# Hyena long convolution: filter quarters in four banks, decays made a step ahead, copies and loads moved

## What is computed

```python
def bidir_long_conv(z, h_fwd, h_bwd, bias):
    L = z.shape[1]
    k = jnp.concatenate([h_fwd, jnp.zeros_like(h_fwd[:1]), h_bwd[1:][::-1]], axis=0)
    kf = jnp.fft.rfft(k.astype(jnp.float32), n=2 * L, axis=0)
    zf = jnp.fft.rfft(z.astype(jnp.float32), n=2 * L, axis=1)
    y = jnp.fft.irfft(zf * kf, n=2 * L, axis=1)[:, :L]
    return (y + z.astype(jnp.float32) * bias).astype(z.dtype)

def hyena_mixer(h, ...):
    u = short_conv(h @ w_in + b_in, conv_w, conv_b)
    x1, x2, v = jnp.split(u, 3, axis=-1)
    filt = hyena_filters(L, ...)          # sin-MLP times exp(-t * |deltas|)
    z = v
    for n, gate in enumerate((x1, x2)):
        z = gate * bidir_long_conv(z, filt[:, n, 0], filt[:, n, 1], fbias[n])
    return z @ w_out + b_out
```

## Time and profile before

| | us |
|---|---|
| median of 3 runs | 3601.22 (3597.62 to 3602.07) |
| the profiled execution, its time | 3599.02 |
| its span, first to last instruction | 3597.4 |
| first matmul of the long convolution | 391.94 |
| first matmul of M(0,0), M(1,0), M(2,0) | 452.80, 567.60, 680.56 |
| third tile of the output projection begins | 1012.12 |

### The profile page before, as it was taken

One profiled execution on the slowest core, in us unless ns is written; L12 is line 12 of the kernel. 1 busy time (PEld: TensorE's weight loads), 2 busy tenths in 40 slices (PEclk: granted clock), 3 DMA queues, 4 the chain that ended last, 5 costly groups with the idle time before them and its releaser, 6 DMA issues.

```text
span 3597.4 us, 49991 instructions
## 1 busy us (share of the span) xinstructions
PE 3287.9 (91%) x19458; PEld 2568.9 (71%) x19458; DVE 2141.1 (60%) x3189; ACT 1304.9 (36%) x2141; POOL 312.3 (9%) x508
## 2 busy tenths in 40 slices
PE   7999788888798999999899889999999979999797
PEld 4888445554576788888687757777777758888685
DVE  6999634343356555554677655555556576665676
ACT  3221333333234433333345443333334253333344
POOL 0111234444200000000000200000000000000000
PEclk8999989998899999999999999999999989999999
DMA  7555644567621322222634410000001133333632
GB/s 290 205 199 200 212 120 137 161 179 153 201 75 59 129 85 80 82 94 105 218 100 144 152 54 8 15 7 7 7 25 59 65 102 106 103 103 111 220 100 88
DMA packets 183696, 410.14 MB, mean 114 GB/s; under 512 B 33263, under 2 KB 60207, under 8 KB 180791
## 3 DMA queue, kind: packets, MB, share of 16 engines
q1 hardware_dynamic: 131288, 270.56, 22.7%
q0 software_dynamic: 51936, 131.27, 12.4%
q10 hardware_dynamic: 288, 5.77, 0.4%
HBM read 262.38 MB, written 81.00 MB: 95 GB/s over the span
## 4 chain that ended last, share of the span: by engine, by line
PE 76%; DVE 12%; DMA 4%; ACT 3%; issue 3%; POOL 1%; SPq 1%; DVEq 0%; ACTq 0%
PE ps L655 19%; PE ps L657 19%; PE ps L656 19%; PE ps L2487 3%; PE ps L2327 3%; PE ps L2461 2%; PE ps L2422 2%; PE ps L2440 2%; PE ps L725 1%; DVE mx L2859 1%; PE ps L2362 1%; PE ps L2522 1%; DMA traw<-hidden_scratch 1%; PE ps L2496 1%; DVE pts L2840 1%
## 5 line engine op out<-in xcount | busy, mean ns | idle before, releaser
L655 PE MATMUL ps<-HB,gsp 128*128 128x512 f32 x1232 | 488.7, 397 | 37.3 <-DVE HB L831 22.0
L656 PE MATMUL ps<-HB,gsp 128*128 128x512 f32 x1232 | 484.9, 394 | 0.0
L657 PE MATMUL ps<-HB,gsp 128*128 128x512 f32 x1232 | 483.7, 393 | 0.0
L1109 DVE TENSOR_TENSOR gsp<-graw,gsp 128x512 fp32r<-128x512 f32 x330 | 226.5, 690 | 262.3 <-ACT gsp L1088 261.5
L1088 ACT ACTIVATE gsp<-graw 128x512 fp32r<-128x512 f32 x330 | 206.6, 628 | 325.5 <-PE ps L657 266.1
L655 PEld LDWEIGHTS ps<-HB,gsp 128*128 128x128 f32 x1232 | 234.3, 190 | 90.6 <-issue 21.5
L655 PE MATMUL ps<-tsp,wdh 128*128 128x512 f32 x616 | 243.6, 396 | 36.6 <-DVE tsp L1366 36.6
L657 PEld LDWEIGHTS ps<-HB,gsp 128*128 128x128 f32 x1232 | 234.1, 190 | 49.9
L656 PEld LDWEIGHTS ps<-HB,gsp 128*128 128x128 f32 x1232 | 234.7, 190 | 46.6 <-issue 1.0
L656 PE MATMUL ps<-tsp,wdh 128*128 128x512 f32 x616 | 242.1, 393 | 0.0
L657 PE MATMUL ps<-tsp,wdh 128*128 128x512 f32 x616 | 242.0, 393 | 0.0
(11 more groups left out here) (278 smaller groups left out, 7498.4 us busy)
## 6 DMA issues: line engine op xcount, KB each, us to landing
graw<-in_w_gu SPq DMA_DIRECT2D x176, 256.0 KB, 2.7
mring<-in_mod_w POOLq DMA_DIRECT2D x78, 512.0 KB, 4.5
hidden_scratch<-R SPq DMA_DIRECT2D x154, 256.0 KB, 2.4
traw<-hidden_scratch SPq DMA_DIRECT2D x154, 256.0 KB, 2.6
t2k<-s POOLq DMA_DIRECT2D x80, 256.0 KB, 5.6
t2z<-s POOLq DMA_DIRECT2D x160, 128.0 KB, 6.0
t2w<-w POOLq DMA_DIRECT2D x160, 128.0 KB, 3.3
wd<-in_w_dx SPq DMA_DIRECT2D x6, 2816.0 KB, 14.7
```

Of the source, the lines that this page charges most:

```text
L655: pe.matmul(o, wh, xh, start=start, stop=False, skip_group_check=onto)
L656: pe.matmul(o, wh, xl, start=False, stop=False, skip_group_check=onto)
L657: return pe.matmul(o, wl, xh, start=False, stop=stop, skip_group_check=onto)
L1109: dve.tensor_tensor(gsp[U % 3][:, 1, :], graw[:, q, W_SLOT[i], :], gsp[U % 3][:, 0, :].bitcast(F32), ALU.subtract).then_inc(w.lo, 1)
```

## The change

- **Four A banks.** The first pair of a K step is in banks 0 and 1, its second pair in 6 and 7. PE waits for the last use of the bank in hand (A_FREE) and no longer for all tiles before a pair. M(it,1) takes its two spectrum sets in the other order (0, 6).
- **Decays ahead.** `dec` has four buffers. ACT makes all four decays of a quarter in the step after the K step before it (B, Z or M), behind the copies that are due there, or, where two K steps follow one another, at the head of the second. In a K step it then copies all held transforms.
- **Order on PE.** In Z steps that find a held filter quarter, two transposes come ahead of the filter's transforms; each signal transform is one place later, and up to two are carried into the next K step. In B steps the held transforms come behind two parts of B, not one.
- **Spectrum copied by two engines.** ACT copies the parts 0 and 2 of S, DVE the parts 1 and 3 (semaphore `s_kd`).
- **Last short convolution.** It moves behind DVE's tiles of K(0,1), the two reductions behind those of K(0,0); of twelve half reductions four stay in K(0,2) and K(0,3), eight go behind S(0,0).
- **Tail.** `mix_raw` is loaded once S(4,1) is computed, ahead of B(4,0); `gbuf` after the weights; the loads of `R` wait until the last `t2w` has landed. Four of the eight `mix_x_low` steps of DVE move into M(4,1).

`mix_raw` goes ahead of `gbuf`. The core of the diff:

```diff
+            for x in range(n["A"], n["A"] + 4 if kind in "KZB" else 0):
+                u = x - n["A"]
+                A_BANK.append(6 * (u // 2) + u % 2 if kind == "K" else u % 2)
+                A_FREE.append(a_last[A_BANK[x]])
+                a_last[A_BANK[x]] = x + 1
...
-        BANK_A, SETS_B = (0, 1), (4, 2)
-        SETS_C, SETS_D, SETS_S = ((4, 2), (6, 0)), ((6, 0), (4, 2)), (4, 6)
+        SETS_B = (4, 2)
+        SETS_C, SETS_D, SETS_S = ((4, 2), (0, 6)), ((6, 0), (4, 2)), (4, 6)
...
+            def decays(quarter):
+
+                it, o = quarter // 4, quarter % 4
+                kb = it if it < NCH else NCH + o
+                act.wait_ge(s_jl[kb % 2], 48 * (kb // 2 + 1))
+                for u in range(4):
+                    ku = 4 * quarter + u
+                    at = NBX + u if it == NCH else ku % 16
+                    if ku >= 4:
+                        act.wait_ge(s_ae, KA_AT[ku - 4] + 1)
+                    act.activation(dec[ku % 4][:], dlt[kb % 2][:, 0:CW], ACT.Exp, scale=nt[:, at:at + 1]).then_inc(s_dec, 1)
...
-                if au >= 2:
-                    pe.wait_ge(s_ae, au - 1)
+                if A_FREE[au]:
+                    pe.wait_ge(s_ae, A_FREE[au])
...
-                        if au:
-                            pe.wait_ge(s_ae, au)
                         bank_a_free(au)
+                        bank_a_free(au + 1)
+                        if p == 1 and o == 0 and it:
+                            pe.wait_ge(s_kd, n["k"] // 2)
...
-                        forward_held(2)
-                        held = [("Z", au, n["B"] + u, 8 * it + 4 * o + u, which)]
+                        if u or not lag:
+                            forward_held(len(held) - (lag // 2 if o or u < 3 else 0))
+                        held.append(("Z", au, n["B"] + u, 8 * it + 4 * o + u, which))
...
+                    dve.wait_ge(s_pr, 8 * (2 * it + o))
+                    for u in (1, 3):
+                        dve.wait_ge(s_kf, n["k"] + u + 1)
+                        dve.tensor_copy(kk[:, 1024 * u:1024 * u + 1024].rearrange("p (a r c) -> p r a c", a=2, r=2),
+                                        pair(SETS_S[1]).rearrange("p r (a c) -> p r a c", a=2)).then_inc(s_kd, 1)
...
+            sp.wait_ge(s_ae, A_END["B", NCH, 0])
+            sp.dma_start(share(gbuf, NCH), u_share(NCH, 1)).then_inc(s_gl, 16)
             sp.wait_ge(s_df, N_Z)
             sp.wait_ge(s_pr, N_Z)
+            sp.wait_ge(s_w1a, 32 * (N_Z // 8))
+            sp.wait_ge(s_w1o, 32 * 7 * (N_Z // 8))
...
-                        mix_x_low(dve, 0, 0, range(KD))
+                        mix_x_low(dve, 0, 0, range(4))
```

More of the change, by code:

```diff
@@ L2693, in short_conv, with tile_end @@
                                          op0=ALU.mult, op1=ALU.add).then_inc(s_u, 1)
-                mods(i, j, first, True)
-            stream_dve(dve, p_in, 24, short_conv, lambda i, j, first: mods(i, j, first, False))
+            def tile_end(i, j, first, last):
+                if not (last and j == 1):
+                    short_conv(i, j, first)
+                    mods(i, j, first, True)
+            stream_dve(dve, p_in, 24, tile_end, lambda i, j, first: mods(i, j, first, False))
             def last_mods(halves):
@@ L2780, in _ @@
                                           .to_broadcast([P, 2, 2, CW]), ALU.mult).then_inc(s_pr, 1)
+                        if tail and 1 <= u < 5:
+                            mix_x_low(dve, 0, 0, range(u + 3, u + 4))
                         if tail and u == 7:
```

94 lines of the change are left out of this document (54 added, 40 removed).

## The result

The change makes the kernel faster, by half of what was forecast:

| | before | changed |
|---|---|---|
| median of the runs | 3599.42 us | 3567.62 us |
| ratio | | 0.9916, 95% interval 0.9898 to 0.9934 |
| profiled execution, span | 3597.4 us | 3563.2 us |
| mean granted clock | 0.956 | 0.963 |

What follows compares the result with a forecast made beforehand. PE's waits for DVE's ksb in the long convolution, and the clock they lower, bound the kernel. Passes 49, start 12, M(4,1) 4 and tail 4 make 69 us: 3599.0 to 3530, as a median 3532 us; range 3508 to 3560.

Steps and rivals of the forecast that it cites:

- the walk: Pass 1 followed step by step with the trace's times: M(1,1) starts at 626.6 instead of 641.22, net 12.2 us a pass.
- What bounds the kernel: Long convolution: PE's filter matmuls wait 49.0 us for DVE's ksb, and idle time in K also lowers the clock.
- The pass: M(1,0) to M(2,0), four times: waits and slow clock in K go, S unchanged; 12.2 us each, 49 in all.
- the first rival: The clock falls in K as before: 4.5 us a pass, 18 in all, 3550 us; chance 0.24.
- The opening of M(it,1): PE waits 5.6 us for t2z: 9.4 us of POOL's sends, then 4.7 to the landing; caps the gain at 14.6.
- The rival that goes with it: t2z lands 3 us earlier and no clock falls in M(1,1): 6 us a pass, 24 in all, 3508; chance 0.14.
- The start: Short convolution and reductions moved behind DVE's tiles: M(0,0) opens at 443.5 instead of 454.91; gain 12 us, 7 if worse.
- M(4,1): mix_raw loaded earlier lets t2z land at 953.4, not 958.29: 4.9 us, less 0.9 for mix_x_low; net 4.0.
- The tail: B(4,1) starts 4 us earlier, loads of R start some 5.7 us later: 4 us of a possible 10, not below -3.
- The slower one: ACT's four decays, 1.8 us, ahead of the first signal copy in five Z steps delay M(it,1): 9 us, 3610; chance 0.03.
- Nothing comes through: POOL's sends cannot come forward, so time won in K is spent waiting at M: between 3594 and 3608; chance 0.04.
- The marks that were to tell: Trace signs such as ksb waits under 15 us, passes of 99 to 103, M(it,1) waits of 4 to 7; wrong above 107.

Runs made afterwards that it cites:

- e_three: Changed kernel with zbuf's load behind t2z's landing, the modulations ahead of DVE's copies, mi and mib ahead of the last store; 3546.06 us, ratio 0.9859.
- t_hold: e_three with POOL waiting until the t2z sends have landed before it issues the t2k sends of K(it+1,2); 3542.06 us, ratio 0.9848.
- t_delay: e_three with ten small DVE instructions (2.0 us) added behind DVE's copies in S(1,1), S(2,1) and S(3,1); 3561.82 us, ratio 0.9903.

## Why the prediction was wrong, point by point

The sum had 69 us, and 34.2 lie between the two spans. The 34.8 that are missing: 20.8 in the four passes, 8.7 at the start, 1.5 at M(4,1), 3.8 in the tail. Three steps of the walk failed: DVE's first tile of K(2,0) (12.1 us in pass 1), the time from the first `t2z` send to M(it,1) (2.4 us a pass), and SP's queue at the start (8 us).

**What bounds the kernel: right.** The waits for `ksb` were the thing to remove; 49.0 us became 2.9 in K (it said under 15), 52.5 became 5.8 in K and B together, and with two banks instead of four it is 47.6 again. That an idle microsecond in K costs more than itself was right too, and stronger than the sum used it.

**The pass, 12.2 us each, 49 in all: 28.2.** S unchanged was right (4.24 us from its first matmul to the first pair of K(2,0), before 4.10). K(2,0) was walked wrong in pass 1: the step "0.3 us for DVE's first tile ... behind its own copy" left out the ten instructions that DVE's new copies push in front of that tile. They make B 2.0 us late, the clock falls to 0.69 (the first rival, its chance 0.24, came true in this pass only, and for a reason it did not name), and 12.1 us are lost in pass 1 as a whole; the modulations in S(2,0), ahead of the second half of B(1,1), have a share in it (3.6). This is the largest single miss, and it is mine, not the chip's: "of a step that is moved or added, who now stands behind it" had been asked of PE and ACT, not of DVE.

**The opening of M(it,1): right in kind, 2 us too early.** The wait stands where it was put. I priced it as 9.4 us of POOL's sends and 4.7 for the landing, 14.1 from the first send. Measured, first send to opening: before the change 17.8, 17.3, 17.1, 16.4; changed 16.6, 16.3, 15.4, 17.9; e_three 14.4, 16.5, 15.9, 15.2; t_hold 14.1, 14.8, 15.4, 14.3. The repetition of the changed kernel has up to 19.5, and one pass of the run on the decays 22.1. Two causes are seen: `zbuf`'s load ahead of the sends, about 1.5 us a pass, and, less surely, the `t2k` sends behind them, 0.7 (15.7 on average in the five profiles without the load, 15.0 in the two that also hold those sends back). What is left is within 1 us of the 14.1. POOL's own time matters less than it seems, since the last landing doesn't follow when the sends go out sooner. In e_three, from 589.0 to 605.5, the view of the DMAs says:

```profile
DMA packets 2038, 3.54 MB, mean 215 GB/s; under 512 B 1177, under 2 KB 1177, under 8 KB 2037
...
q0 software_dynamic: 2037, 3.53, 86.6%
```

They are busy for 87% of that time with POOL's sends alone, so that the engines and not POOL set the pace there is likely, but argued. The small packets are not the reason: the 1177 under 512 B are of 16 B and less, together 0.01 of the 3.54 MB and 5% of the packets' time, and the other packets are of 4 KB. The term is 2.4 us a pass too small in the changed kernel, 10 us in all. The walk had come out right for pass 1 (626.6, measured 625.95) by two errors against each other: pass 0 had moved everything 11.9 us ahead, and K(2,0) and the slots lost it again.

The Trainium skill, page DMA: Bandwidth & Descriptors, section Anatomy of one DMA — SWDGE (gpsimd) path, would give 2.3 us for a send of 128 KB, an estimate by its rule for a single DMA. The trace doesn't agree for these bursts: of the 160 sends of the changed kernel the shortest takes 2.8 us from issue to landing, the median is 4.5, and the last one ahead of M(it,1) takes 3.4 to 7.8. The rival that goes with it, an early landing with 3508, needed 1.7 us from the end of the last send to M; the shortest in the changed kernel is 3.1, and in t_hold, with nothing sent behind, it is 3.9 to 5.9.

**The start, 12: 3.3 at the first product.** Two errors. The price of the moved reductions was seen and right. (The walk's own times, 443.5 against 454.91, give 11.4, not 12.) What was missed is that the moved convolution takes SP's store with it, and behind that store `mi` and `mib`: 2.6 MB were issued 16 us later, into the landing of the last `t2k`. Put ahead again, S(0,0) and the first product come at 426.39 and 443.93, where the walk had them (427 and 443.5). The step of the walk was sound and one queue was left out, SP's; that the two times fit to within 1 us is partly luck, given the 425.7 to 432.2 of the later runs.

**M(4,1), 4.0: 2.5.** It opens 15.6 us behind the first send, before the change 18.3; if all of that is the load of `mix_raw` in the way, it was worth 2.7, not 4.9; no run moves it alone. The step that failed is the landing: 7.0 us behind the last send, not 4.7 (9.6 before).

**The tail, 4: 2.6 at the third tile, 0.2 by the end.** The two sides of the exchange were named (B earlier, `R` later) and nearly cancel: B runs in 7.26 us as guessed and the third tile waits 13.3 us for `R`. What of the 2.6 reaches the end can't be seen under a scatter of 4 us.

**The rivals.** The slower one, ACT's decays ahead of the signal copies, was tested and costs nothing that shows. "Nothing comes through" didn't happen, though M(it,1) takes part of each gain.

**The marks that were to tell.** Waits for `ksb` under 15: yes. Passes of 99 to 103: 104.1, 114.4, 100.5, 105.5, one of four; the one above 107 is the mark "wrong", and it pointed at the right place. Clock 1.0 from B(1,0) on: no, 0.69. M(it,1) waits 4 to 7: two of four, 5.93 and 5.13, the others 2.10 and 8.53. M(4,1) at 953 less what was won before: 2.4 us later than that. S unchanged: yes. B(4,1) no longer waits for `t2w`: yes.

**The range** ended at 3560, 10 us above the case of the fallen clock. Without the one or the other omission the time would have come out inside, by these prices (3556 or 3560); the two and the late openings (10 us) together lie outside. The two omissions (12 and 8 us) are both of one sort, an instruction or a load that stands behind a moved or added one on its own queue.

## What to carry to other kernels

When work is given to an engine, list what stood behind that place on the same engine and who waits for it, and do the same for the queue that stores a moved result: both misses here were instructions that nobody moved. Where a stretch of dense matmuls follows a short wait, price the wait with the clock behind it (2.0 us became 4.4 to 7.7 here), not by its length. And where many transfers must land before a stage opens, take the time from the first send to the opening as one measured number with its spread (14 to 22 us in single passes here), and look for loads that run beside them. Before a difference at one place of two traces is called an effect, look how far two traces of the same program differ there.

## What was unexpected of the hardware

- 2.0 us more of idle time ahead of B decide over the clock of the next 16 us: 0.22 us of idle leaves it at 1.00 (pass 2), 2.25 us takes it to 0.69 in the changed kernel and 2.26 to 0.68 in t_delay; the same 32 matmuls take 3.76 or 7.06 us (5.88 and 6.58 in the other two passes of t_delay). PE had waited 0.36 and 0.58 us ahead of either.
- Sends that go out sooner need not bring the opening nearer: in one pass they are out in 9.4 us instead of 11.8, and M opens 16.7 us behind the first instead of 16.3. M(it,1), fed by 16 sends of 128 KB, 2.1 MB, opened 14.1 to 19.5 us behind the first in all passes read but one (22.1), and one load of 1 MB issued just ahead of them costs about 1.5 us.
- Two traces of one program lie far apart at the same matmul: M(4,1) opens at 924.28 and 934.09 in the changed kernel, at 899.60 and 909.70 in two runs that differ only behind it. A difference of 10 us there, read from one trace each, shows nothing.
